# Experts with the tokens stationary on 64- and 32-wide column tiles and the weights streaming past them

## The reference

```python
def expert_choice_ffn(x, w_router, w_gate, w_up, w_down):
    cap = CAP_FACTOR * T // N_EXPERTS          # 64 sample tokens, 16 prompt tokens
    aff = jax.nn.softmax((x @ w_router).astype(jnp.float32), -1)
    gsel, idx = lax.top_k(jnp.swapaxes(aff, 1, 2), cap)
    xs = x[bidx, idx]
    hdn = jax.nn.silu(jnp.einsum('becd,edf->becf', xs, w_gate)) * jnp.einsum('becd,edf->becf', xs, w_up)
    out = jnp.einsum('becf,efd->becd', hdn, w_down) * gsel[..., None].astype(x.dtype)
    return jnp.zeros_like(x).at[bidx, idx].add(out)
```

## Time and profile before

| | |
|---|---|
| median of three runs | 3255.63 us |
| span of the profiled execution, first to last instruction | 3254.3 us |
| TensorE busy | 3039.7 us, 93% of the span |
| TensorE weight loads busy | 2229.6 us, 69% |
| VectorE / ScalarE / GpSimd busy | 963.2 / 577.3 / 96.0 us |
| bytes moved by DMA | 545.5 MB, 168 GB/s over the span |

### The profile page before, as it was taken

One profiled execution on the slowest core, in us unless ns is written; L12 is line 12 of the kernel. 1 busy time (PEld: TensorE's weight loads), 2 busy tenths in 40 slices (PEclk: granted clock), 3 DMA queues, 4 the chain that ended last, 5 costly groups with the idle time before them and its releaser, 6 DMA issues.

```text
span 3254.3 us, 43264 instructions
## 1 busy us (share of the span) xinstructions
PE 3039.7 (93%) x18405; PEld 2229.6 (69%) x18405; DVE 963.2 (30%) x2408; ACT 577.3 (18%) x1297; POOL 96.0 (3%) x145
## 2 busy tenths in 40 slices
PE   6999999797999999997999989999986999999994
PEld 1465479745887777771456459999944888777773
DVE  1100136643001000102177536666645010001002
ACT  3100111240000000003167212222242000000002
POOL 0000000000000000000000000000000000000000
PEclk9899998897999999998999999999997999999997
DMA  8411100217999999957411100000016899999992
GB/s 281 154 52 52 45 1 1 65 62 270 312 311 303 303 309 308 306 183 271 155 52 52 39 0 1 1 2 1 1 65 224 279 314 304 307 305 307 306 310 87
DMA packets 276365, 545.50 MB, mean 168 GB/s; under 512 B 15233, under 2 KB 23817, under 8 KB 276233
## 3 DMA queue, kind: packets, MB, share of 16 engines
q1 hardware_dynamic: 175049, 328.64, 29.4%
q10 hardware_dynamic: 93600, 188.75, 16.6%
q0 software_dynamic: 7584, 26.22, 3.2%
HBM read 517.89 MB, written 25.70 MB: 167 GB/s over the span
## 4 chain that ended last, share of the span: by engine, by line
PE 88%; DVE 6%; ACT 3%; DMA 2%; issue 1%; SPq 0%; DVEq 0%; POOL 0%; ACTq 0%
PE ps L1204 28%; PE ps L1215 14%; PE ps L803 8%; PE ps L813 6%; PE ps L760 5%; PE ps L1139 3%; PE ps L1101 3%; PE ps L804 2%; PE ps L1083 2%; PE ps L880 1%; PE ps L1115 1%; PE ps L791 1%; PE ps L950 1%; PE ps L966 1%; ACT L424 1%; ACT L423 1%
## 5 line engine op out<-in xcount | busy, mean ns | idle before, releaser
L1204 PEld LDWEIGHTS ps<-wk,slots 128*128 128x128 f32 x6144 | 691.1, 192 | 16.5 <-issue 16.0
L1204 PE MATMUL ps<-wk,slots 128*128 128x80 f32 x6144 | 689.9, 275 | 0.0
L1215 PE MATMUL ps<-qkv,og 128*80 128x512 f32 x1024 | 446.7, 594 | 2.4 <-DVE og L1748 1.3
L1215 PEld LDWEIGHTS ps<-qkv,og 128*80 128x80 f32 x1024 | 151.0, 150 | 275.5 <-issue 268.0
L803 PE MATMUL ps<-hT,slots 128*128 128x512 f32 x640 | 334.0, 604 | 3.1 <-ACT hT L455 3.1
L1204 PE MATMUL ps<-wk,qkv 128*128 128x80 f32 x2048 | 233.9, 275 | 0.0
L1204 PEld LDWEIGHTS ps<-wk,qkv 128*128 128x128 f32 x2048 | 231.3, 192 | 0.0
L804 PEld LDWEIGHTS ps<-hT,slots 128*128 128x128 f32 x640 | 123.5, 193 | 156.6 <-issue 156.6
L813 PE MATMUL ps<-slots,hT 128*128 128x512 f32 x480 | 209.3, 596 | 0.0
L760 PE MATMUL ps<-slots,cnd 128*2 128x512 f32 x384 | 172.0, 602 | 35.1 <-DVE x L1776 24.1
L1724 DVE COPY idc<-idT 80x1 uint32 (+1 forms) x32 | 4.8, 149 | 612.8 <-DMA moe_d<-og,idc 612.7
(11 more groups left out here) (261 smaller groups left out, 3228.5 us busy)
## 6 DMA issues: line engine op xcount, KB each, us to landing
slots<-in_w_gate_dram ACTq DMA_DIRECT2D x60, 2048.0 KB, 9.2
qkv<-in_w_down_dram SPq DMA_DIRECT2D x34, 2048.0 KB, 9.8
slots<-in_w_up_dram SPq DMA_DIRECT2D x32, 2048.0 KB, 10.2
qkv<-in_w_up_dram SPq DMA_DIRECT2D x32, 2048.0 KB, 7.8
qkv<-in_w_down_dram ACTq DMA_DIRECT2D x30, 2048.0 KB, 7.8
slots<-in_w_ada_dram SPq DMA_DIRECT2D x24, 2048.0 KB, 8.1
slots<-in_w_in_dram SPq DMA_DIRECT2D x16, 2048.0 KB, 8.1
slots<-in_w_out_dram SPq DMA_DIRECT2D x4, 2048.0 KB, 16.2
```

The source lines that it names most:

```text
L1204: ins = mm(PS[:, j, fb * CAP:(fb + 1) * CAP], slot[j][:, kt, fb * P:(fb + 1) * P], xsT[q][:, kt, :], start=(kt == 0), stop=(kt == KT - 1))
L1215: ins = mm(PS[0:CAP, 4 + j, :], hdT[:, ft, :], slot[4 + j][:, ft, :], start=(ft == 0), stop=(ft == KT - 1))
```

## The change

**Slots** hold half the contraction and all 1024 output columns of a matrix, in rows of 4 KB (`wide`, four contraction steps each): gate k0-3, up k0-3, gate k4-7, up k4-7, down k0-3, down k4-7. All six loads are issued by SyncE, against a semaphore `moe_free` with four counts an expert.

**Gate and up** (`gate_up`) have the tokens stationary. The 64 sample tokens go onto two column tiles of 64, one for each half of the output columns, 512 columns moving. The 16 prompt tokens (with 16 sample tokens as padding) go onto four column tiles of 32, 256 columns moving. The sample pass and then the prompt pass run over the first half of the contraction, then both over the second.

**The hidden values** now lie with tokens on partitions. They are transposed back on TensorE (four transposes for the sample, two for the prompt) and copied out by ScalarE. `down_sample` and `down_prompt` work like `gate_up`. The transposes of the next expert's tokens stay between gate/up and down.

**Scatter.** The sample result is scattered as 128 rows of 2 KB (two for each token) to `moe_s`, the prompt result as 128 rows of 1 KB (four for each token) to `moe_p`; 64 of the prompt rows are padding and go to 64 spare rows. Index columns for gather, sample scatter and prompt scatter and the two columns of weights are built on VectorE in a tensor `pick5`, turned with five transposes and copied back in four pieces.

```diff
-            return a[name][L].rearrange("e (k p) n -> e p k n", p=P)[e, :, :, hf * HC:(hf + 1) * HC]
+            return a[name][L].rearrange("e (k p) n -> e p k n", p=P)[e, :, 4 * hf:4 * hf + 4, :]
...
-                    for j in range(6) if first else (1, 3, 5):
-                        if not first:
-                            sp.wait_ge(S("moe_used"), L * PER["moe_used"] + e * 6 + (j - 5))
-                        sp.dma_start(slot[j], w_expert(L, e, j)).then_inc(land[j], 16)
+                    for j in range(6):
+                        if not first and j not in (1, 3):
+                            sp.wait_ge(S("moe_free"), L * PER["moe_free"] + e * 4 + ((1, 1, 2, 2, 3, 4)[j] - 4))
+                        sp.dma_start(wide[j], w_expert(L, e, j)).then_inc(land[j], 16)
...
-                    pool.wait_ge(S("o_ready"), L * PER["o_ready"] + e * 2 + 2)
+                    held = 3 * EX * L + (3 * EX - 2) if e is EX - 1 else e * 3 + (3 * EX * L + 2)
+                    pool.wait_ge(S("os_ready"), L * PER["os_ready"] + e + 1)
                     if not first:
-                        pool.wait_ge(S("scattered"), L * PER["scattered"] + e * 16)
-                    hold(2 * EX * L + (2 * EX - 1) if e is EX - 1 else e * 2 + (2 * EX * L + 2))
-                    pool.indirect_dma_start(moe_d, bass.IndirectOffsetOnAxis(ap=idc[q][0:CAP, :], axis=0),
-                                            osb[q][0:CAP, :], None, compute_op=ALU.add).then_inc(S("scattered"), 16)
+                        pool.wait_ge(S("scattered"), L * PER["scattered"] + e * 32)
+                    hold(held)
+                    pool.indirect_dma_start(moe_s, bass.IndirectOffsetOnAxis(ap=idc[q][1][:, :], axis=0),
+                                            osS[q], None, compute_op=ALU.add).then_inc(S("scattered"), 16)
+                    pool.wait_ge(S("op_ready"), L * PER["op_ready"] + e + 1)
+                    hold(held + 1)
+                    pool.indirect_dma_start(moe_p, bass.IndirectOffsetOnAxis(ap=idc[q][2][:, :], axis=0),
+                                            osP[q], None, compute_op=ALU.add).then_inc(S("scattered"), 16)
...
+                    act.wait_ge(S("gu_s"), L * PER["gu_s"] + e + 1)
+                    A(ebS, PS[:, 0, :], ACT.Tanh, scale=0.5).then_inc(S("gexp"), 1)
+                    act.wait_ge(S("moe_free"), L * PER["moe_free"] + e * 4 + 2)
+                    A(ebP, PS[:, 2, 0:256], ACT.Tanh, scale=0.5).then_inc(S("gexp_p"), 1)
+                    act.wait_ge(S("hs_turned"), L * PER["hs_turned"] + e + 1)
+                    A(hdS, PS[:, 3, :], ACT.Copy).then_inc(S("hs_in"), 1)
+                    act.wait_ge(S("hp_turned"), L * PER["hp_turned"] + e + 1)
+                    A(hdP, PS[:, 5, 256:512], ACT.Copy).then_inc(S("hp_in"), 1)
+                    act.wait_ge(S("down_s"), L * PER["down_s"] + e + 1)
+                    if first is None:
+                        act.wait_ge(S("scattered"), L * PER["scattered"] + (e - 1) * 32)
+                    A(osS[q], PS[:, 4, :], ACT.Copy, scale=gsc[q][:, 0:1]).then_inc(S("os_ready"), 1)
+                    act.wait_ge(S("moe_free"), L * PER["moe_free"] + e * 4 + 4)
+                    A(osP[q], PS[:, 5, 0:256], ACT.Copy, scale=gsc[q][:, 1:2]).then_inc(S("op_ready"), 1)
...
+                def gate_up(e, q):
+
+                    pe.wait_ge(S("xs_in"), L * PER["xs_in"] + e + 1)
+                    for j in (0, 2):
+                        for i in range(2):
+                            pe.wait_ge(land[j + i], e * 16 + (16 * moe_base(L, j + i) + 16))
+                        for k in range(4):
+                            kt = 2 * j + k
+                            for i in range(2):
+                                for c in range(2):
+                                    ins = mm(PS[c * 64:(c + 1) * 64, i, :], xsT[q][:, kt, 0:CAPS],
+                                             wide[j + i][:, k, c * HC:(c + 1) * HC], start=(kt == 0), stop=(kt == KT - 1))
+                        if j:
+                            ins.then_inc(S("gu_s"), 1)
+                        for k in range(4):
+                            kt = 2 * j + k
+                            for i in range(2):
+                                for c in range(4):
+                                    ins = mm(PS[c * 32:(c + 1) * 32, 2, i * 256:(i + 1) * 256], xsT[q][:, kt, CAP - 32:CAP],
+                                             wide[j + i][:, k, c * 256:(c + 1) * 256], start=(kt == 0 and i == 0),
+                                             stop=(kt == KT - 1), skip_group_check=True)
+                        ins.then_inc(S("moe_free"), 1)
+
+                def hidden_turn(e):
+
+                    pe.wait_ge(S("hid_s"), L * PER["hid_s"] + e + 1)
+                    for k in range(4):
+                        ins = tr(PS[:, 3, k * P:(k + 1) * P], ebS[:, k * P:(k + 1) * P], ident)
+                    ins.then_inc(S("hs_turned"), 1)
+
+                def down_sample(e, first):
+
+                    pe.wait_ge(S("hs_in"), L * PER["hs_in"] + e + 1)
...
+                    for hf in range(2):
+                        pe.wait_ge(land[4 + hf], e * 16 + (16 * moe_base(L, 4 + hf) + 16))
+                        for k in range(4):
+                            ft = 4 * hf + k
+                            for c in range(2):
+                                ins = mm(PS[c * 64:(c + 1) * 64, 4, :], hdS[:, k * P + hf * 64:k * P + hf * 64 + 64],
+                                         wide[4 + hf][:, k, c * HC:(c + 1) * HC], start=(ft == 0), stop=(ft == KT - 1))
+                        if hf == 0:
+                            pe.wait_ge(S("hid_p"), L * PER["hid_p"] + e + 1)
...
+                            for k in range(2):
+                                t2 = tr(PS[:, 5, 256 + k * P:256 + (k + 1) * P], ebP[:, k * P:(k + 1) * P], ident)
+                            t2.then_inc(S("hp_turned"), 1)
+                    ins.then_inc(S("down_s"), 1)
+
+                def down_prompt(e):
+
+                    pe.wait_ge(S("hp_in"), L * PER["hp_in"] + e + 1)
+                    for hf in range(2):
+                        for k in range(4):
+                            ft = 4 * hf + k
+                            for c in range(4):
+                                ins = mm(PS[c * 32:(c + 1) * 32, 5, 0:256],
+                                         hdP[:, (ft % 2) * P + (ft // 2) * 32:(ft % 2) * P + (ft // 2) * 32 + 32],
+                                         wide[4 + hf][:, k, c * 256:(c + 1) * 256], start=(ft == 0), stop=(ft == KT - 1),
+                                         skip_group_check=True)
+                        ins.then_inc(S("moe_free"), 1)
...
+                def expert(e, q, first=False, last=False):
+
+                    gate_up(e, q)
+                    hidden_turn(e)
+                    if not last:
+                        turn(e + 1, 1 - q, False)
+                    down_sample(e, first)
+                    down_prompt(e)
...
+                sample, prompt = idx[:, 0:CAPS], idx[:, CAPS:CAP]
+                V.tensor_scalar(pick5[:, 0, 0:CAPS], sample, float(P), None, ALU.add)
+                V.tensor_copy(pick5[:, 0, CAPS:CAP], prompt)
+                for c in range(2):
+                    V.tensor_scalar(pick5[:, 1, c * 64:(c + 1) * 64], sample, 2.0, float(c), ALU.mult, ALU.add)
+                    V.tensor_copy(pick5[:, 3, c * 64:(c + 1) * 64], vals[:, 0:CAPS])
+                for c in range(4):
+                    V.tensor_scalar(pick5[:, 2, c * 32 + CAPP:(c + 1) * 32], prompt, 4.0, float(c), ALU.mult, ALU.add)
+                    ins = V.tensor_copy(pick5[:, 4, c * 32 + CAPP:(c + 1) * 32], vals[:, CAPS:CAP])
+                ins.then_inc(S("topk"), 1)
```

More of the change, by code:

```diff
@@ L88, in backbone @@
         slot = [s.rearrange("p (k n) -> p k n", k=KT) for s in SL]
+        wide = [s.rearrange("p (k n) -> p k n", k=4) for s in SL]
         wk = sb("wk", [P, 4608])
@@ L675, in experts @@
                 A(aff[:, :, :], aff[:, :, :], ACT.Exp).then_inc(S("sme"), 1)
-                def expert(e, q, first, last=False):
-                    def load(j):
-                        if not last:
-                            act.dma_start(slot[j], w_expert(L, e + 1, j)).then_inc(land[j], 16)
-                    for hf in range(2):
-                        act.wait_ge(S("moe_used"), L * PER["moe_used"] + e * 6 + (2 * hf + 1))
-                        if first != 0:
-                            act.wait_ge(S("hidden"), L * PER["hidden"] + e * 2 + (hf - 1))
-                        A(eb[hf], PS[:, 2 * hf, 0:320], ACT.Tanh, scale=0.5).then_inc(S("gexp"), 1)
-                        load(2 * hf)
-                    for hf in range(2):
-                        act.wait_ge(S("moe_used"), L * PER["moe_used"] + e * 6 + (5 + hf))
-                        if hf == 0 and first is None:
-                            act.wait_ge(S("scattered"), L * PER["scattered"] + (e - 1) * 16)
```

(31 more changed lines are left out.)

119 lines of the change are left out of this document (65 added, 54 removed).

## The result

The changed kernel takes 2960.35 us (median of 4 runs, 2958.45 to 2968.35) against 3257.01 for the kernel before on the same chip: a ratio of 0.9096, 95% interval 0.9081 to 0.9112.

A forecast was written before the change was run, and what follows sets the result against it. TensorE was taken to bound the experts: 32.7 + 1.4 + 1.35 + 0.3 + 0.9 = 36.6 us each, taken as 38.0. Span 3254.3 - 163 + 8, plus 1.3, gave 3101 us; own range 3020 to 3180, widened to 3420.

The forecast's parts named there:

- the margin for limits that meet: Per expert: 38.0 us taken where TensorE's terms sum to 36.6, for limits that jitter against each other.
- the floor of the transfers: Expert loads: 32.5 us for six slots at 387 GB/s, with gathers and scatters 35.5 to 38.2 us an expert.
- Sample passes: TensorE, per expert: 20.9 us with two tiles overlapping wholly, plus 0.9 for one tile running alone at four pass ends.
- Prompt passes: TensorE, per expert: 192 records at 0.061 us, the pace of the solver's 64x64 matmuls, 11.8 us as a floor.
- Transposes 1.4, nine changes of shape 1.35, a wait of 0.3: TensorE, per expert: token and hidden-value transposes, tile shape changes at 0.15 each, waiting for the turned hidden values' copy.
- Three limits of 35.5 to 38.2: Per expert: TensorE 36.6 us, transfers 35.5 to 38.2 and the scatter-to-gather loop 35.6 jitter against each other, giving 38.0.
- Whether 4 KB rows move faster than 2 KB rows no row shows; 0 is taken: Expert loads: no gain was counted for longer rows, so the rate stayed at 387 GB/s, 32.5 us.
- No slack is left: Scatter, pick, gather: gather lands 22 us after the expert's start, against a turn at about 23; nine us slack before.
- Fixed costs, +8: Outside the expert periods: token choice and the layer's end cost 4 us more a layer, 8 in all.
- Rival A: TensorE queue: a matmul's two records block it, at most two overlap; 47.2 us an expert, 3396 us; chance 0.30.

The follow-up runs named there:

- e3: The changed kernel with gate and up's prompt pass on two column tiles of 64 in place of four of 32; 3162 us.
- e5: The changed kernel with only the first of four contraction steps of each slot loaded, from the second expert on; 2953 us.
- e6: The changed kernel with one contraction step of four in each half of the prompt's down pass; 2951 us.
- e4: The changed kernel with each slot loaded in two transfers of 1 MB, in rows of 2 KB in place of 4 KB; 3001 us.
- e2: The changed kernel with gate and up's prompt pass reordered: two matmuls (four records) on one tile, then the next tile; 2958 us.
- e10: The changed kernel with gate and up's prompt pass reordered: four matmuls (eight records) on one tile, then the next tile; 3242 us.
- e1: The changed kernel with gate and up's prompt pass reordered: eight matmuls (16 records) on one tile, then the next tile; 3458 us.
- e9: The changed kernel without column tiles: all 80 tokens stationary on the whole array, prompt passes left out but for one small matmul each; 3371 us.
- e7: The changed kernel with gate and up's two sample passes first and both prompt passes behind them; 3089 us.

## Why the prediction was wrong

The direction and the main mechanism were right: TensorE was the bound, tiles overlap wholly, and the transfers come next. The size was not: 38.0 us an expert was forecast and 33.8 is measured, 4.2 x 32 = 134 of the 141 us missed; the rest is the fixed costs. Two steps failed most. One is the margin for limits that meet, 1.4 us on top of the sum of 36.6. The other is the floor of the transfers, 35.5 to 38.2 us where 34.05 is measured, with the rows of 4 KB put at nothing: it set the lower end of the range, 3020, and would have held the forecast at 35.5 even with every TensorE term right. The terms:

- *Sample passes, 20.9 + 0.9.* Measured 2 x 7.02 + 2 x 3.59 = 21.2, of which four changes of shape are 0.4: 20.8. The two tiles' records start 0.007 us apart all through a pass, so no tile runs on alone at its end.
- *Prompt passes, "192 x 0.061 = 11.8 us is my floor".* Measured 3 x 3.59 = 10.8, of which three changes are 0.3: 10.5. The pace of the 64x64 matmuls was that of one tile, not a floor for issue; the records of the four tiles start 0.007 us apart. The lower bound of 10.5, by columns streamed over four tiles, was the right one.
- *Transposes 1.4, nine changes of shape 1.35, a wait of 0.3.* All together 33.69 - 20.8 - 10.5 = 2.4: 0.9 for the changes at 0.10 each (e3), 1.5 for transposes and wait, of which the wait is 0.13. The 0.15 that I read from the earlier trace rows held the ordinary spacing of 0.06 too, and I multiplied it by nine without subtracting that.
- *"Three limits of 35.5 to 38.2 that jitter against each other: I take 38.0."* TensorE needs 33.69 (e5), the transfers 34.05 (e6), and together they need 34.0 from the ninth period of the first layer on and 33.8 on average. Six slots decouple them, so here two limits close together cost the larger of the two and not more, and less while the lead lasts.
- *Transfers, "Whether 4 KB rows move faster than 2 KB rows no row shows; 0 is taken".* They do: 30.7 us at 410 GB/s in place of 32.5. Scatters and gathers take 9.8% of 33.9, 3.3 us, within my 3.0 to 5.7 and near the lower end. e4 puts 40 us on the rows.
- *Scatter, pick, gather, "No slack is left".* 3.9 us are left. The chain takes 17.8 from the expert's start, not 22: the evacuation of a prompt result is short, the scatter issues in 1.56 and not 2.3, and its 7.5 us to land start at the issue, while I added 8 from its end.
- *Fixed costs, +8.* TensorE's gap at the choice of tokens grew by 0.9 us a layer (21.64 for 20.75) and not by 3: I priced operations that don't wait for each other by their length (0.18) and not by their distance (0.07 to 0.11). From the first of them to the first expert it is 1.1 and 2.6 us more in the two layers. The end of the last layer, from the last copy to the first sum, got shorter, 14.3 for 15.5, where I had +1. The span fell by 297.6 us and 32 periods by 297, so all fixed parts together came to about nothing.

Rival A, at 0.30, was the wrong idea of the queue: e3 has a slower pass on two tiles than the changed kernel has on four, and e2 and e10 show how many records a tile takes. What the Trainium skill states in "TensorE: Matmul & The Clock Gate" in its section on packing, a strict program order of matmul starts, does not hold as it stands for these fp32 matmuls: in e1 the next tile begins before the last three records of the run ahead of it have started. The stream does stop for all tiles, but only with a fifth record for one of them.

The range, as far as it was the forecast's own, ended at 3020 because the bounds of single terms were not carried through: with 20.9 + 10.5 + 1.4 for TensorE and an open lower end for rows that no trace had priced it would have reached 2960. That is said with the result in hand.

## What to carry to other kernels

Few stationary columns are a reason for column tiles: in fp32 two tiles of 64 and four of 32 gave their whole factor here, as long as no more than four records (two matmuls) in a row went to the same tile. When two resources are decoupled by buffers, start from the larger of the two; here it needed no margin for their meeting. That holds only while buffers are released early enough: once the transfers were near their limit, a release 7 us later closed a loop that cost 129 us. Price a row of operations by the distance between starts in the trace and not by the length of one, and a change of kind by what it adds to that distance.

## What was not expected of the hardware

- A column tile takes four fp32 matmul records, the running one among them, before the instruction stream stops for the others: from runs of 16 the last four overlap (e1), from runs of 8 the last four (e10), from runs of 4 all (e2).
- Loads in rows of 4 KB ran at 409 to 413 GB/s and in rows of 2 KB at 386 to 387, on one queue and with nothing else to do (742 to 750 us in all traces; 2 MB a transfer, 1 MB in e4 alone).
- A change of column tile shape between passes costs 0.10 us (the sample pass of e3 against that of the changed kernel).
- An indirect scatter of 128 rows, of 1 or 2 KB each, takes GpSimd 1.56 us and one of 80 rows of 4 KB 1.44.
- Behind waits of 2.0 us (e9) and 2.4 to 2.8 us (e7) TensorE's granted clock fell to 1.2 GHz for part of what followed, in most periods but not in all (0.80 over 943.50 to 952.00 in e9).
